# The late modulation weights of two transformer blocks moved from the routings to the middle of the output projections

## The reference

```python
    # mod = silu(c) @ w_ada[l] + b_ada[l], cut into six rows of 1024: shift, scale, gate (mixing), shift, scale, gate (experts)
    h_lat = h_lat + mod_lat[2] * y_lat                       # y_lat: output projection of the mixer, y @ w_out
    u2 = modulate(rms_norm(h_lat, g_ffn[l]), mod_lat[3], mod_lat[4])
    h_lat = h_lat + mod_lat[5] * expert_choice_ffn(u2, w_router[l], w_gate[l], w_up[l], w_down[l])

def expert_choice_ffn(h, w_router, w_gate, w_up, w_down):
    cap = max(1, (EC_CAPACITY * n) // N_EXPERTS)             # 32 tokens for each expert
    aff = jax.nn.softmax((h @ w_router).astype(jnp.float32), axis=-1)
    g, idx = lax.top_k(jnp.swapaxes(aff, 1, 2), cap)
    xe = jax.vmap(lambda hb, ib: hb[ib])(h, idx)
    y = jnp.einsum('becf,efd->becd', jax.nn.silu(xe @ gate) * (xe @ up), w_down) * g[..., None]
```

## Time and profile before

| | us |
|---|---|
| median of 3 runs | 2658.14 |
| the runs | 2652.57 to 2658.61 |
| span of the profiled execution | 2650.8 |

### The profile page before, as it was taken

How to read it: one execution, slowest core, us unless ns; L and a number is a source line. 1 busy time by engine, 2 the same in 40 slices (tenths; PEclk the granted TensorE clock), 3 DMA queues, 4 the chain that set the end, 5 groups by cost and what they waited for, 6 DMA issues and landing times.

```text
span 2650.8 us, 27230 instructions
## 1 busy us (share of the span) xinstructions
PE 2516.9 (95%) x11522; PEld 1546.7 (58%) x11522; DVE 1183.6 (45%) x1973; ACT 437.3 (16%) x877; POOL 92.6 (3%) x69
## 2 busy tenths in 40 slices
PE   9999999889999999987879999999999999999999
PEld 5344343424368833332338857888866875878884
DVE  4971221212165521110127756546657665553665
ACT  2111110001132210000011101531101111260110
POOL 0011000000000000000001100001001100001000
PEclk9999999999999999999999999999999999999999
DMA  9753999999961589999996553324453644333441
GB/s 371 324 221 133 404 427 425 428 428 427 425 277 64 222 367 427 426 428 427 426 424 222 177 186 133 114 98 186 159 186 148 191 175 159 127 106 133 165 181 68
DMA packets 90598, 690.06 MB, mean 260 GB/s; under 512 B 25316, under 2 KB 27748, under 8 KB 29164
## 3 DMA queue, kind: packets, MB, share of 16 engines
q1 hardware_dynamic: 87984, 682.66, 64.5%
q0 software_dynamic: 848, 2.90, 0.3%
q10 hardware_dynamic: 1644, 2.76, 0.3%
HBM read 687.22 MB, written 1.06 MB: 260 GB/s over the span
## 4 chain that ended last, share of the span: by engine, by line
PE 82%; DMA 13%; DVE 5%; issue 1%; ACT 0%; SPq 0%; POOL 0%; DVEq 0%; POOLq 0%
PE bank L766 79%; DMA ring<-in_stream 9%; DMA ring_high<-in_stream 3%; PE bank L769 3%; DVE ab_z L2292 1%; DVE moe_turned L2484 0%; DVE moe_silu L2482 0%; DVE moe_results L2488 0%; DVE ring L2716 0%; DVE hidden L2798 0%; DVE normed L2668 0%; DVE hidden L2751 0%; SPq L739 0%; POOL ab_ln_sum L3020 0%; DVE hidden L2836 0%
## 5 line engine op out<-in xcount | busy, mean ns | idle before, releaser
L766 PE MATMUL bank<-normed,ring 128*128 128x256 f32 (+1 forms) x1824 | 493.7, 427 | 8.4 <-DVE normed L2668 4.5
L766 PEld LDWEIGHTS bank<-normed,ring 128*128 128x128 f32 x1824 | 341.7, 190 | 154.6 <-issue 105.6
L766 PE MATMUL bank<-ring,gates 128*128 128x256 f32 (+1 forms) x1504 | 378.0, 396 | 3.8 <-DVE ring L2716 2.8
L766 PE MATMUL bank<-ring,moe_chosen 128*64 128x512 f32 x1504 | 334.5, 595 | 29.0 <-DMA ring<-in_stream 27.4
L766 PEld LDWEIGHTS bank<-ring,gates 128*128 128x128 f32 x1504 | 284.4, 191 | 62.9 <-issue 23.0
L766 PE MATMUL bank<-ring,normed 128*128 128x256 f32 (+1 forms) x1376 | 314.1, 375 | 0.5 <-DVE cd_rinv L2535 0.5
L766 PEld LDWEIGHTS bank<-ring,normed 128*128 128x128 f32 x1376 | 256.0, 190 | 36.8 <-issue 2.3
L766 PEld LDWEIGHTS bank<-ring,moe_chosen 128*64 128x64 f32 x1504 | 105.3, 137 | 245.9 <-issue 190.4
L2482 DVE TENSOR_TENSOR moe_silu<-bank,moe_silu 128x512 f32<-128x512 f32 x32 | 22.1, 692 | 406.9 <-PE bank L766 406.9
L766 PE MATMUL bank<-ring,moe_turned 128*64 128x512 f32 (+1 forms) x832 | 165.1, 547 | 19.7 <-DVE moe_turned L2484 18.0
L766 PE MATMUL bank<-ring,ffn_hidden 128*128 128x512 f32 x352 | 170.6, 592 | 0.0
(11 more groups left out here) (403 smaller groups left out, 2430.3 us busy)
## 6 DMA issues: line engine op xcount, KB each, us to landing
ring<-in_stream SPq DMA_DIRECT2D x138, 2048.0 KB, 24.6
ring<-in_stream SPq DMA_DIRECT2D x264, 1024.0 KB, 5.4
ring_low<-in_stream SPq DMA_DIRECT2D x10, 2048.0 KB, 36.6
ring_high<-in_stream SPq DMA_DIRECT2D x10, 2048.0 KB, 37.4
ring_far<-in_stream SPq DMA_DIRECT2D x9, 2048.0 KB, 34.6
hidden<-in_stream SPq DMA_DIRECT2D x10, 1024.0 KB, 35.9
normed<-in_stream SPq DMA_DIRECT2D x10, 1024.0 KB, 38.8
ring_filter_freq<-in_stream SPq DMA_DIRECT2D x6, 1024.0 KB, 14.9
```

The costliest lines, as they stand in the source:

```text
L766: return nc.tensor.matmul(o, lhsT, rhs, start=start, stop=stop, skip_group_check=True)
```

## The change

The late weights move in the stream: they stand behind chunk 1 of the output projection, ahead of chunks 2 and 3. PE uses all four quarters there, after the fourth of the eight blocks, once DVE has copied the routers' shift. DVE does this copy after block 1 and no longer at the start of the routing. In layer 1 the quarters go into bank 1, columns 256 to 511, beside the shift, and no longer into bank 3, which the projection uses at that time. In the routings PE has none of these matmuls any more.

```diff
@@ chunk_plan
     for c in range(KB // 2):
         add(("out_ab", c), a["w_out_ab"][0][:, 256 * c:256 * c + 256])
-    ada(1, 1)
+        for q in LATE_QUARTERS.get(c, ()):
+            ada_quarter(1, 1, q)
...
     for c in range(KB // 2):
         add(("out_cd", c), a["w_out_cd"][0][:, 256 * c:256 * c + 256])
-    ada_section(1, 5)
+        for q in LATE_QUARTERS.get(c, ()):
+            ada_section_quarter(1, 5, q)
...
+LATE_QUARTERS, WINDOW_QUARTERS = {1: (0, 1, 2, 3)}, ()
@@ section_of
-    return 3, (3, 2 * P), M.moe[1].ada_row, M.moe[1].ada_turned
+    return (1, T), (3, 2 * P), M.moe[1].ada_row, M.moe[1].ada_turned
@@ tensor_program, project_back
                 ins.then_inc(*(ring.free(name) if half else done.up((tag, "back", n))))
+            for q in LATE_QUARTERS.get(c, ()):
+                pe.wait_ge(*V.at((f"moe{l}", "shift")))
+                section_part(5, q) if l else ada_part(1, 1, q)
@@ tensor_program, moe
-        if l == 0:
-
-            pe.wait_ge(*V.at((tag, "shift")))
-            ada_part(1, 1, 0)
         pe.wait_ge(*V.at((tag, "affinity")))
...
-        if l == 0:
-            ada_part(1, 1, 1)
-            ada_part(1, 1, 2)
-        else:
-            for q in range(KB // 2):
-                section_part(5, q)
         pe.wait_ge(*V.at((tag, "slots")))
...
-        if l == 0:
-            ada_part(1, 1, 3)
-        else:
+        if l:
             section_turn(5)
@@ vector_program, back
+            if n == 1:
+
+                dve.wait_ge(*TE.at((f"moe{l}", "shift")))
+                v.tensor_copy(M.moe[l].shift, bank[SHIFT_BANK[l]][:, 0:len(streams) * NE]).then_inc(*done.up((f"moe{l}", "shift")))
@@ vector_program, moe
-        dve.wait_ge(*TE.at((tag, "shift")))
-        v.tensor_copy(m.shift, bank[SHIFT_BANK[l]][:, 0:R]).then_inc(*done.up((tag, "shift")))
```

More of the change, by code:

```diff
@@ L214, in ada_quarter @@
             add(("ada", l, pair, h, q), a["w_ada"][l, 2 * P * q:2 * P * (q + 1), D * (2 * pair + h):D * (2 * pair + h + 1)])
-    def ada(l, pair):
-        for q in range(KB // 2):
-            ada_quarter(l, pair, q)
     def experts(l):
@@ L246, in chunk_plan, with ada_section_quarter @@
         add(("out_ab", c), a["w_out_ab"][0][:, 256 * c:256 * c + 256])
-    ada(1, 1)
-    def ada_section(l, sec):
-        for q in range(KB // 2):
-            add(("ada_section", l, sec, q), a["w_ada"][l, 2 * P * q:2 * P * (q + 1), D * sec:D * sec + D])
+        for q in LATE_QUARTERS.get(c, ()):
+            ada_quarter(1, 1, q)
+    def ada_section_quarter(l, sec, q):
+        add(("ada_section", l, sec, q), a["w_ada"][l, 2 * P * q:2 * P * (q + 1), D * sec:D * sec + D])
+    for q in WINDOW_QUARTERS:
+        ada_quarter(1, 1, q)
     experts(0)
-    ada_section(1, 4)
+    for q in range(KB // 2):
+        ada_section_quarter(1, 4, q)
     for c0 in (512, 768, 0, 256, 1024, 1280, *(conv_chunk(*x) for x in CONVS)):
@@ L562, in section_of @@
     if sec == 4:
-        return 2, (3, 0), M.ada_row[:, 0:2 * P], M.ada_turned[:, 1, 0:8 * NS]
-    return 3, (3, 2 * P), M.moe[1].ada_row, M.moe[1].ada_turned
+        return (2, 0), (3, 0), M.ada_row[:, 0:2 * P], M.ada_turned[:, 1, 0:8 * NS]
+    return (1, T), (3, 2 * P), M.moe[1].ada_row, M.moe[1].ada_turned
 def turned_of(M, l, pair):
@@ L820, in section_part @@
         name = ("ada_section", 1, sec, q)
-        tile, b = ring.tile(name), section_of(M, sec)[0]
+        tile, (b, at) = ring.tile(name), section_of(M, sec)[0]
         pe.wait_ge(*ring.landed(name))
@@ L825, in section_part @@
             for j in range(4):
-                ins = mm(bank[b][32 * j:32 * j + 32, 0:2 * P], M.cond[:, k, :], tile[:, kk, 2 * P * j:2 * P * j + 2 * P], k == 0, k == KB - 1)
+                ins = mm(bank[b][32 * j:32 * j + 32, at:at + 2 * P], M.cond[:, k, :], tile[:, kk, 2 * P * j:2 * P * j + 2 * P], k == 0, k == KB - 1)
         ins.then_inc(*ring.free(name))
@@ L1761, in section_row @@
         act.wait_ge(*S.chunk.at(("ada_section", 1, sec, KB // 2 - 1)))
-        b, _, row, _ = section_of(M, sec)
-        nc.scalar.copy(row, bank[b][:, 0:2 * P]).then_inc(*done.up(("section_row", sec)))
+        (b, at), _, row, _ = section_of(M, sec)
+        nc.scalar.copy(row, bank[b][:, at:at + 2 * P]).then_inc(*done.up(("section_row", sec)))
     def section_turned(sec):
```

## The result

| | before | after |
|---|---|---|
| median | 2653.45 | 2665.52 |
| the runs (5 each) | 2652.57 to 2658.61 | 2662.10 to 2669.45 |
| span of the profiled execution | 2650.8 | 2662.0 |

The ratio of after to before is 1.0042, with an interval of 1.0030 to 1.0054: slower by 12.1 us in the medians and by 11.2 us in the spans. The two runs of before that were added to the three in the front lowered its median from 2658.14 to 2653.45.

A forecast was written before the change was run, and what follows sets the result against it. Both expert stages were taken as bound by weight transfers in a DMA queue that never empties. Transfers 4.9 us later in layer 0 and 5.1 in layer 1 make 10.0, added to 2658.1: 2668.1 us, range 2659 to 2674.

The forecast's parts named there:

- Parts 1 and 4: Late weights ahead of projection chunks 2 and 3, and DVE's shift copy after block 1: both cost 0.
- Part 2: Late matmuls in the projections, where PE is the bound: projections end 7.2 us later in layer 0, 3.7 in layer 1.
- Part 3: Quarters leaving the routings: 2.2 us come back in layer 0, nothing in layer 1; gathers start 5.0 and 3.7 us later.
- The rival by which the routing gives everything back: All 7.2 and 3.7 us come back in the routings, first gathers start where they did: 2656.3; chance 0.15.
- Part 5: PE idle in the new routings, so low clock on gather and first expert products: 1.7 us in each layer.
- Part 6: From gather to DMAs: first expert issues 6.7 and 5.4 us later, transfers 4.9 and 5.1 us later.
- the backlog: Transfers already queued at layer 0's first expert issues: swallows 1.8 us of PE's 6.7 us delay; 0.3 in layer 1.
- the four early pairs: Layer 0 chunk pairs issued at 228.6 to 234.0 instead of from 266.6 on; ring then full, lead not kept.
- The kept lead: Rival: layer 0's expert stage starts from transfers landed some 20 us sooner, total down to 2629; chance 0.04.
- No low clock: Rival: gathers run without a low clock, 6.6 us slower in all, 2664.7; chance 0.12.
- The long low clock: Rival: 6.8 us of low clock on each gather costs 3.4 us twice, 2671.5; chance 0.12.

The follow-up runs named there:

- one-quarter runs: Kernel before with only layer 0's quarter 0 moved: behind the second projection chunk, ratio 1.0003, or right behind the last projection matmul, ratio 1.0000.
- filled_less: Changed kernel plus a few unread matmuls in PE's routing waits (3 and 2 in layer 0, 3 and 0 in layer 1): ratio 1.0040, span 2658.8.
- e2_layer1: The change in layer 1 alone, layer 0 as in the kernel before: ratio 1.0016, span 2658.9.
- ffn_only: Kernel before with three unread matmuls ahead of the first transpose group of each later feed-forward step: ratio 1.0037, span 2661.9.
- hidden_only: Kernel before with three unread matmuls ahead of the seventh transpose group of each layer's first feed-forward step: ratio 0.9984, span 2649.1.
- order_only: Kernel before with DVE's four down-projection sums moved behind the seventh hidden of a feed-forward step: ratio 0.9954, median 2641.49.
- e4_few: Changed kernel with most late modulation matmuls left out, 4 of 32 kept per layer, tiny ones freeing the other chunks: ratio 1.0010, span 2654.7.
- quarter_in_gap: Kernel before with only layer 0's quarter 0 moved right behind the last projection matmul, shift's copy after block 1: ratio 1.0000, span 2652.3.
- gap_and_order: Kernel before with quarter_in_gap's and order_only's edits together: ratio 0.9952, median 2641.03.

## Why the prediction was right, and where it wasn't

**Sign and size.** Slower by 0.4%, as forecast; 2668.1 was given, 2665.52 measured. Two errors partly cancel in that, which is luck: the sum was 10.0 us where the medians give 12.1 and the spans 11.2, and the median it was added to was 4.7 us higher than that of the wider set of runs.

**Parts 1 and 4** (order of the stream, the shift's copy, both at 0). Right: no wait for a transfer and none for the copy stands in the projection. PE has only its old 0.97 us behind the last block.

**Part 2** (7.2 and 3.7 us): 7.07 and 3.66 us.

**Part 3** (2.2 us come back in layer 0, none in layer 1). Right: the gather was forecast at 280.4 and is at 280.26. In layer 1 it comes 10.44 us later, 6.34 of which are layer 0's, so 4.1 where I had 3.7; the affinities' and slots' transposes ran at low clock too, which I had not counted. The rival by which the routing gives everything back is out, and the one-quarter runs say why: only quarter 0 had stood in the way.

**Part 5** (the clock, 1.7 us each). The mechanism was right and the term mis-sized in layer 0. From the gather to the first issue it took 11.81 us, before 284.92 − 275.35 = 9.57: 2.24 us. In layer 1 962.22 − 953.51 = 8.71 against 7.10: 1.6. I had taken the shorter low stretch that the rows showed, 3.4 us; the real ones were 17 and 13 us long, and what limited the price was only that most of each fell on idle time. The bound was wrong in kind: a low stretch isn't priced by its length but by PE's work inside it. The Trainium skill, page "TensorE: Matmul & The Clock Gate", Part 1, says that an idle TensorE is put to 1.2 GHz and has to work for a while before it gets 2.4. The traces agree: 0.50 through both waits, and 1.00 again some way into the gather; in filled_less, where matmuls lie in these waits, the gathers take 3.81 and 2.23 us.

One reading under this part was wider than its one trace. "It had risen again when the gathers began" is so in the trace of before. Four later traces keep PE's first routing as it was (e2_layer1, ffn_only, hidden_only, order_only), and in all four the clock is low on part of that gather, which takes 4.38 to 4.70 us instead of 3.81. This is e2_layer1's:

```profile
275.61 4.69 PE L769 MATMUL bank<-moe_hot,normed 128*128 128x128 f32 x32
```

From the gather to the first issue these four need 10.1 to 10.5 us, where before's trace has 9.57. Against them layer 0's price of the clock is 1.3 to 1.7 us, not 2.24; the gather of layer 1 takes 2.23 us in all of them but e2_layer1, whose second routing is the changed one.

**Part 6** (from the gather to the DMAs: the backlog swallows 1.8 us, then 0.3). This is the step that was off. The first issue is 7.15 us late and the end of the stage 6.34: 0.8 swallowed, not 1.8. The start was as worked out: with the DMAs empty, line L744's rows (issues in a window, then the time from issue to landing) have

```profile
L744 SPq DMA_DIRECT2D ring_filter_freq<-in_stream x1: 328/328/328, 292.1 to 292.1; - x1
...
DMA to landing us min/median/max: 6.2/6.2/6.2
...
DMA to landing us min/median/max: 5.7/6.7/7.8
```

The first chunk of the first pair landed at 298.3 (forecast 299.3), the second half of the second pair at 298.0 + 7.8 = 305.8 (forecast 305.0), against 300.1 before: 5.7 us late at that point. The rest was lost in the next 60 us with the queue full: chunk for chunk, the landings lag 5.7 us behind before's at 310, 6.2 at 326 and 6.4 from 370 on. In all runs with the four early pairs the swallowed part is 0.5 to 1.1 us: 0.8 in after, 1.0 with layer 0 alone, 1.1 with the late matmuls left out, 0.9 and 0.5 with the filling. The landing that ends the stage differs by up to 1.8 us between traces that have the same first routing (712.5 to 714.3), so one such number is good to a us at most. Five say the same, but all five are taken against the one trace of before, and that one was slow here: from the first issue behind an expert product to the stage's last landing it needs 428.8 us, the four other traces with its routing 428.0 to 428.4, and the five with the early pairs 427.6 to 428.3. By the means of five and five, 428.3 and 427.9, the backlog swallows only 0.4 us. So the term was mis-sized because the backlog of 1.8 us was read from one landing of one trace; what makes this time differ from trace to trace, and why the queue doesn't keep all that it had swallowed by 310 us, stays open. In layer 1 it is 5.71 − 5.48 = 0.2, forecast 0.3.

**The rivals.** The kept lead is out: the DMA share of 285 to 292 is 0.00, and e4_few bounds the worth of the early transfers at 1.1 us. No low clock is out, and filled_less shows what it would have been: 4.4 us at the end of layer 0 and 8.5 behind layer 1. The long low clock happened in length but not in price.

## What to carry to other kernels

Work that stands in another engine's wait is free, and moved to where its own engine is the bound it costs its full time, here 7.07 us for 2.2; of several pieces in a wait, move only the one that someone waits behind. Before moving anything, read the groups of instructions for idle time ahead of a step and look what the awaited engine did just before: four sums of 5.8 us that nobody needed yet cost about as much as this change, and putting them one step later gave 0.46%. Bringing transfers forward gives nothing beyond the room to hold them: the ring was full by 272 us, and the DMAs stood still for the rest.

## What the runs showed of the hardware

**A short idle time of PE that may or may not cost clock.** The 3.3 to 4.1 us in the feed-forward steps (1484 and 2112) left the clock at 1.00 in one trace and put it to 0.50 in another of the same or nearly the same program: behind the first of them 16 matmuls took 3.62 us in before and after, 6.19 in quarter_in_gap and 6.09 in ffn_only; behind the second 5.30 us in before, 5.58 in after and 3.62 in filled_less, there behind 3.93 us of idle time. The runs of before range over 9.5 us (2649.3 to 2658.8 in 17 beside the last three kernels); with the idle time filled over 4.7 us (12 runs), and with it gone over 2.4 us (5 runs of order_only) and 2.8 us (5 of gap_and_order). The time follows the clock in these 17 runs: the five below 2652 us had a mean granted clock of 0.997 or 0.998, the five above 2655.5 us one of 0.993 to 0.995. I take it that these idle times make most of the spread of this kernel. That isn't shown: a range grows with the number of runs, and no more than five stand behind each of the last two numbers.

**What such an idle time costs.** Together the two cost 7.2 us of waiting (by order_only), and behind them the clock 1.7 us in before and 5.8 in ffn_only (2.9 at either place: 1.09 and 6.09 us instead of 0.66 and 3.62, and nearly the same again). A difference of a few us between two traces far behind a change should first be looked for there, before it is put down to the change.
